# Building the bias table of a neighbourhood attention by transfers through a DRAM scratch and one GpSimd addition, in place of small matmuls

## The reference, cut to what matters

```python
s_loc = jnp.einsum('bhrcqd,bhrcwkd->bhrcqwk', q_blk, k_nb).astype(jnp.float32) * scale
roff = row_idx - r[:, None] + (WIN_ROWS - 1)
coff = jnp.clip(kcol - qcol[:, :, None], -(WIN_COLS - 1), WIN_COLS - 1) + (WIN_COLS - 1)
bias = rpb[:, roff[:, None, None, :, None], coff[None, :, :, None, :]]
s_loc = jnp.where(valid[:, :, None, :], s_loc + bias[None].astype(jnp.float32), NEG_INF)
```

## Time and profile before

| | |
|---|---|
| Median of 3 runs | 1601.49 us (1594.64 to 1602.89) |
| Span of the profiled execution | 1598.6 us |
| PE busy | 1559.7 us, 98% of the span, 8269 matmul records |
| DVE busy | 1197.9 us, 75% |
| ACT busy | 962.1 us, 60% |
| POOL busy | 15.0 us, 1% |
| DMA | 463.38 MB, mean 290 GB/s |
| Mean granted TensorE clock | 0.982 of full speed |

### The profile page before, as it was taken

One profiled execution on the slowest core, in us unless ns is written; L12 is line 12 of the kernel. 1 busy time (PEld: TensorE's weight loads), 2 busy tenths in 40 slices (PEclk: granted clock), 3 DMA queues, 4 the chain that ended last, 5 costly groups with the idle time before them and its releaser, 6 DMA issues.

```text
span 1598.6 us, 21590 instructions
## 1 busy us (share of the span) xinstructions
PE 1559.7 (98%) x8269; PEld 1283.9 (80%) x8269; DVE 1197.9 (75%) x1055; ACT 962.1 (60%) x781; POOL 15.0 (1%) x28
## 2 busy tenths in 40 slices
PE   7999999999999999999999999999999999999997
PEld 3975679899958878888888888888888888888886
DVE  3755457555557578888888888888888888888886
ACT  3422155433444477777777767767767767776774
POOL 1000000000000000000000000000000000000000
PEclk9899999999999899999999999999999999999998
DMA  9745767755546479989989989998999998998990
GB/s 326 253 145 175 239 208 239 251 197 186 183 158 211 158 249 375 374 302 366 368 301 366 373 314 352 370 346 324 376 335 326 375 364 294 370 372 308 370 365 29
DMA packets 221826, 463.38 MB, mean 290 GB/s; under 512 B 7572, under 2 KB 48696, under 8 KB 221768
## 3 DMA queue, kind: packets, MB, share of 16 engines
q1 hardware_dynamic: 220984, 460.84, 80.7%
q0 software_dynamic: 784, 1.75, 0.4%
HBM read 460.98 MB, written 1.57 MB: 289 GB/s over the span
## 4 chain that ended last, share of the span: by engine, by line
PE 94%; DVE 2%; ACT 2%; DMA 1%; issue 0%; SPq 0%; DVEq 0%; ACTq 0%
PE ps L417 92%; PE ps L815 2%; DVE w_lo L1161 1%; ACT hT L1006 1%; DMA raw<-in_ada_w 1%; PE ps L511 1%; DVE rstd L1231 0%; ACT arena L1118 0%; DVE w_lo L1474 0%; ACT w_hi L978 0%; PE ps L594 0%; DVE xT L1481 0%; ACT rnd L1011 0%; DVE tok L1203 0%; SPq L899 0%
## 5 line engine op out<-in xcount | busy, mean ns | idle before, releaser
L417 PE MATMUL ps<-w_hi,rnd 128*128 128x512 f32 x2720 | 868.5, 396 | 2.1 <-DVE rnd L1468 2.1
L1474 DVE TENSOR_TENSOR w_lo<-raw,w_hi 128x2048 fp32r<-128x2048 f32 x335 | 763.5, 2290 | 133.2 <-ACT w_hi L1075 132.7
L1075 ACT ACTIVATE w_hi<-raw 128x2048 fp32r<-128x2048 f32 x336 | 643.5, 1918 | 195.6 <-PE ps L417 195.6
L417 PEld LDWEIGHTS ps<-w_hi,rnd 128*128 128x128 f32 x2720 | 511.8, 188 | 112.7 <-issue 2.3
L417 PE MATMUL ps<-w_lo,rnd 128*128 128x512 f32 x1360 | 530.4, 390 | 0.0
L417 PEld LDWEIGHTS ps<-w_lo,rnd 128*128 128x128 f32 x1360 | 256.1, 188 | 53.3
L417 PE MATMUL ps<-rnd,w_hi 128*128 128x256 f32 x1632 | 293.9, 285 | 4.1 <-DVE rnd L1242 1.7
L417 PEld LDWEIGHTS ps<-rnd,w_hi 128*128 128x128 f32 x1632 | 255.0, 194 | 9.0 <-DVE rnd L1242 3.6
L1161 DVE TENSOR_TENSOR w_lo<-raw,w_hi 128x2048 fp32r<-128x2048 f32 x77 | 175.8, 2285 | 97.9 <-ACT w_hi L978 97.8
L978 ACT ACTIVATE w_hi<-raw 128x2048 fp32r<-128x2048 f32 x77 | 146.6, 1913 | 152.2 <-PE ps L417 143.7
L417 PE MATMUL ps<-rnd,w_lo 128*128 128x256 f32 x816 | 230.5, 282 | 0.0
(11 more groups left out here) (131 smaller groups left out, 717.2 us busy)
## 6 DMA issues: line engine op xcount, KB each, us to landing
raw<-in_moe_w SPq DMA_DIRECT2D x336, 1024.0 KB, 6.9
raw<-in_ada_w SPq DMA_DIRECT2D x48, 1024.0 KB, 5.5
raw<-in_ffn_w SPq DMA_DIRECT2D x33, 1024.0 KB, 5.4
raw<-in_w_in SPq DMA_DIRECT2D x12, 1024.0 KB, 10.5
raw<-in_w_out SPq DMA_DIRECT2D x4, 1024.0 KB, 5.7
raw<-in_fourier_w SPq DMA_DIRECT2D x4, 1024.0 KB, 5.0
out<-tok SPq DMA_DIRECT2D x4, 256.0 KB, 2.1
arena<-dft_constants POOLq DMA_DIRECT2D x1, 640.0 KB, 8.0
```

Source lines behind the costliest of these rows:

```text
L417: return pe.matmul(out, lhsT, rhs, start=first, stop=last, **kw)
L1075: act.activation(w_hi[:, slot, :], raw[:, m % RAW, :], ACT.Copy).then_inc(hi_done, 1)
L1474: dve.tensor_tensor(w_lo[:, slot, :], raw[:, m % RAW, :], w_hi[:, slot, :].bitcast(F32), ALU.subtract).then_inc(lo_done, 1)
```

## The change

The 24 rows of `rpb` no longer go through SBUF and TensorE. GpSimd issues one transfer from DRAM to a DRAM scratch `bias_rows`, which holds the 3 x 31 values of each head 65 times in a row. Then four transfers read it with a row step of 92 elements in place of 93, so that each query column begins one element further to the left, and write the table's four quarters (64 query columns x 8 heads x 64 key columns each) to `bias`. GpSimd waits for them, adds the mask to the whole table in one instruction, and gives `bias_ready`, for which DVE waits in `soften(0)`. TensorE and DVE lose five turns each, `rpbT`, `rpb_rows` and `diag` go, and the router's loads have waits of their own. In the diff the line numbers are left out.

```diff
-CONSTS = [..., ("diag", 2 * GRID_W - 1), ("pair_sum", NG)]
+CONSTS = [..., ("pair_sum", NG)]
+BIAS_COPIES = GRID_W + 1
+    bias_rows = nc.dram_tensor("bias_rows", (HEADS, BIAS_COPIES, BIAS_ROWS * BIAS_COLS), F32, kind="Internal")
```

On TensorE:

```diff
-        def bias_table(q):
-            b = bank()
-            pe.wait_ge(evac_done, rpb_turn)
-            for i in range(16):
-                kc = 16 * q + i
-                last = mm(b[0:GRID_W, 24 * i:24 * (i + 1)], diag[:, GRID_W - 1 - kc:2 * GRID_W - 1 - kc], rpbT[:],
-                          True, True)
-            done(last)
         transposes([kc_tok[:, i * P:(i + 1) * P] for i in range(4)])
-        pe.wait_ge(in_small, 16 * (HEADS + 2))
-        transposes([rpb_rows[:]])
-        rpb_turn = turn[0]
         ada_turn(0, 2, 3)
-        bias_table(0)
-        bias_table(1)
         project("win", h_r, chunk_ready=h_chunk)
-        bias_table(2)
-        bias_table(3)
         project("win", h_r)
         pe.wait_ge(h_ready, 4 * KT)
+        pe.wait_ge(in_small, 32)
```

On GpSimd:

```diff
-        for h in range(HEADS):
-            pool.dma_start(rpb_rows[BIAS_ROWS * h:BIAS_ROWS * (h + 1), :],
-                          ins["rpb"][0, h, WIN_ROWS - 2:WIN_ROWS + 1, :]).then_inc(in_small, 16)
+        rows, row = 2 * WIN_ROWS - 1, BIAS_ROWS * BIAS_COLS
+        near = bass.AP(ins["rpb"].tensor, (WIN_ROWS - 2) * BIAS_COLS,
+                       [[rows * BIAS_COLS, HEADS], [0, BIAS_COPIES], [1, row]])
+        pool.dma_start(bias_rows.ap(), near).then_inc(bias_copied, 16)
         pool.dma_start(router[:], ins["router_w"][0].rearrange("(k p) e -> p k e", p=P)).then_inc(in_small, 16)
         pool.dma_start(router_bias[:], ins["router_b"][0:1, :].to_broadcast([P, EXPERTS])).then_inc(in_small, 16)
+        pool.wait_ge(bias_copied, 16)
+        for qr in range(GRID_R):
+            for kr in range(GRID_R):
+                window = bass.AP(bias_rows, (kr - qr + 1) * BIAS_COLS + WIN_COLS - 1,
+                                 [[row - 1, GRID_W], [BIAS_COPIES * row, HEADS], [1, GRID_W]])
+                pool.dma_start(bias[qr * GRID_W:(qr + 1) * GRID_W, :, kr * GRID_W:(kr + 1) * GRID_W],
+                               window).then_inc(in_bias, 16)
+        pool.wait_ge(in_const, 16)
+        pool.wait_ge(in_bias, 16 * GRID_R * GRID_R)
+        pool.tensor_tensor(bias, bias, mask.rearrange("p (o k) -> p o k", o=1).to_broadcast([P, HEADS, P]),
+                           ALU.add).then_inc(bias_ready, 1)
         round_h(0)
```

On VectorE:

```diff
-        def bias_table(q):
-            b = full()[:, 0:384].rearrange("p (k h r) -> p h k r", h=HEADS, r=BIAS_ROWS)
-            for qr in range(GRID_R):
-                rows = slice(qr * GRID_W, (qr + 1) * GRID_W)
-                for kr in range(GRID_R):
-                    cols = slice(kr * GRID_W + 16 * q, kr * GRID_W + 16 * q + 16)
-                    m = mask[0:GRID_W, cols].rearrange("p (o k) -> p o k", o=1).to_broadcast([GRID_W, HEADS, 16])
-                    last = dve.tensor_tensor(bias[rows, :, cols], b[0:GRID_W, :, :, kr - qr + 1], m, ALU.add)
-            last.then_inc(evac_done, 1)
-        copy_turn(rpbT[:], lambda b: b[0:BIAS_COLS, 0:24])
-        bias_table(0)
-        bias_table(1)
         for c in range(4):
             copy_turn(qT[:, c, :], lambda b: b[:, 0:T])
-        bias_table(2)
-        bias_table(3)
         def soften(h):
+            if h == 0:
+                dve.wait_ge(bias_ready, 1)
             dve.wait_ge(sc_full, h + 1)
```

More of the change, by code:

```diff
@@ L61 @@
 CONSTS = [("ident", P), ("ones", P), ("mask", P), ("earlier", P), ("slot_ids", SLOTS), ("expert_ids", EXPERTS),
-          ("diag", 2 * GRID_W - 1), ("pair_sum", NG)]
+          ("pair_sum", NG)]
 DFT_CONSTS = [("dft_pos", 2 * P), ("dft_cos", 2 * FGC), ("dft_sin", 2 * FGC)]
@@ L191, in _build @@
     router_bias = sb("router_bias", [P, EXPERTS])
-    rpb_rows = sb("rpb_rows", [HEADS * BIAS_ROWS, BIAS_COLS])
-    rpbT = sb("rpbT", [BIAS_COLS, HEADS * BIAS_ROWS])
     small = sb("small", [P, 176])
@@ L259, in _build @@
     ident, ones, mask, earlier = C("ident"), C("ones"), C("mask"), C("earlier")
-    diag = C("diag")[0:BIAS_COLS]
     dft_pos = DFT("dft_pos")
@@ L291, in _build @@
     whole_used = sem("whole_used")
-    in_vec, in_const, in_x, in_cache, in_small, in_dft = (
-        sem(n) for n in ("in_vec", "in_const", "in_x", "in_cache", "in_small", "in_dft"))
+    in_vec, in_const, in_x, in_cache, in_bias, in_small, in_dft = (
+        sem(n) for n in ("in_vec", "in_const", "in_x", "in_cache", "in_bias", "in_small", "in_dft"))
+    bias_copied, bias_ready = sem("bias_copied"), sem("bias_ready")
     mm_done = sem("mm_done")
@@ L1428, in _ @@
         b = full()
+        dve.wait_ge(in_small, 32)
         dve.tensor_tensor(logits, b[:, 0:16].rearrange("p (g e) -> p g e", g=NG),
@@ L1607, in shape_constants @@
     put("expert_ids", np.tile(np.arange(EXPERTS), (P, 1)))
-    u = np.arange(2 * GRID_W - 1)
-    z = (np.arange(BIAS_COLS)[:, None] + u[None, :] == WIN_COLS - 1 + GRID_W - 1).astype(np.float32)
-    put("diag", z)
     angle = 2 * np.pi * (np.outer(i, i) % P) / P
```

## The result

The changed kernel takes 1620.69 us (median of 4 runs, 1616.65 to 1623.9) against 1601.89 us for the kernel before: 1.0138 times as long in the comparison of the runs, with an interval of 1.0107 to 1.0169 (1.0117 by the two medians). The forecast of 1600.5 us and its range to 1611 are missed. The profiled execution has a span of 1619.1 us, 20.5 more than before.

A forecast was written before the change was run, and what follows sets the result against it. TensorE was taken to set the pace, so a shift at the start carries to the end. Terms -4.0 - 1.3 + 0.4 - 0.1 - 1.1 + 4.8 + 0.3 = -1.0 us gave 1600.5 us, range 1595 to 1611.

The forecast's parts named there:

- From there on all is shifted by about -1 us.: Behind L704's successor, everything to the end was to keep its duration and only move by about -1 us.
- the named places: Weight landings, first projection's start, clock between the first two projections, additions near L704's successor: where the forecast would show.
- Second block: Table matmuls at 66.95 to 70.92, ahead of the next projection: removing them counts in full, -4.0 us.
- clock behind it: Projection after the second table matmuls: 12 matmul records no longer run at the lower clock, -1.3 us.
- First block: Table matmuls at 45.90 to 52.2, inside the first norm: covered by the norm's late chunks, so 0.
- clock +0.4: First projection: idle TensorE may keep the clock low longer, 0 to +2.0 us, taken as +0.4.
- Bank rotation: At L704, five turns fewer: TensorE waits for four of VectorE's additions instead of eight, -1.1 us.
- Transfers: At the start, copy (2.5) and windows (0.6 x 4.4) delay the second split half's landing: +4.8 us, ends +1.9 and +9.5.
- GpSimd's addition: Mask addition of 128 x 1024 elements, ending about 42, may slow VectorE's subtractions: 0 to +2.2 us, taken +0.3.
- The late table: Rival: windows land after about 48, so GpSimd's first rounding and the norm wait: +12, 1613 us; chance 0.14.
- The start is not delayed: Rival: small packets fit between weight packets, transfers cost 0.5 and the sum is -5.3: 1596 us; chance 0.10.
- The addition holds VectorE: Rival: a subtraction beside GpSimd's addition waits for all of it, up to 2.5 us: 1603 us; chance 0.06.

The follow-up runs named there:

- e9: Changed kernel plus two unused tensors (512 and 224 bytes), so that every remaining tensor lies at its byte in the kernel before: 1598.99 us, 1.0006.
- e10: e9 with the copy, its windows and the addition issued behind GpSimd's first four roundings instead of ahead of them: 1592.44 us, 0.997.
- e3: Changed kernel with the copy, its windows and the addition behind GpSimd's first four roundings instead of ahead of them: 1613.06 us, 1.0089.
- e4: e3 with an unused tensor of 32 bytes per partition ahead of arena and rnd: 1597.3 us, 0.9983.
- e5: e3 with 224 unused bytes per partition ahead of arena and rnd, so rnd begins 64 past a multiple of 256: 1593.44 us, 0.9964.
- e11: e9 with the scratch's 64 copies (not 65) outermost and its 8 heads inside: 1600.69 us, 1.0004.
- e7: e3 with 160 unused bytes per partition ahead of arena and rnd, so rnd begins at a multiple of 256: 1612.78 us, one run.
- e16: e10 with only the dense stages' regions of rnd 32 bytes further on, at 96 past a multiple of 256: 1598.36 us, 0.9993.
- e12: e9 with the copy still at the start, but the windows and the addition behind GpSimd's first four roundings: 1594.87 us, 0.9984.

## Why the prediction was wrong

**The step that failed** is none of the sum's terms but a sentence behind it: "From there on all is shifted by about -1 us." It took for granted that matmuls that the change doesn't touch keep their duration. With `diag`, `rpb_rows` and `rpbT` gone, the operand of 6528 of the 8140 records had moved. The missing term is +21.7 us (1620.69 against e9's 1598.99). Most of it is in the expert stage, which no edit touches: 15.4 us by the two traces (1021.9 against 1006.5 us from its first record to its last). The prediction named the sign of this: a span more than 8 us off that the named places don't explain. The sum itself holds for e9, where nothing has moved: forecast -1.0 us, measured 1.0006, which is +1.0 us with an interval of -1.3 to +3.0.

Its terms one by one, against e9 where the place would blur them:

- *Second block -4.0, clock behind it -1.3:* right, but half given back by the next term. From the start of the first projection to the next transposes it took 36.26 us before, 32.94 after, 33.05 in e9: -3.2 with the next term, where -4.9 was put down. No stretch between the two projections is at 1.2 GHz now: e9 is at 1.00 from 70 on.
- *First block 0, clock +0.4:* the block was covered, but the clock was mis-sized. With TensorE idle in its place, it stayed at the lower level until the first projection was under way. e10, whose transfers come late, has the same (0.50 in 58.6 to 61), so it isn't their doing. Here is the kernel before by stretch (PE, PEld, DVE, ACT, POOL, then the clock), from the start of its first projection:

```profile
58.00:61.00 3.00, 2.86 (x25) 2.77 (x25) 2.91 (x10) 1.52 (x1) 0.00 (x0) 1.00 0.25 95
61.00:64.00 3.00, 3.00 (x29) 3.00 (x28) 2.43 (x4) 1.92 (x1) 0.00 (x0) 1.00 0.10 21
```

  and e9, whose first projection starts at 63.07:

```profile
57.00:63.00 6.00, 5.19 (x18) 4.26 (x18) 3.90 (x11) 5.91 (x16) 1.21 (x3) 0.50 1.04 369
63.00:66.00 3.00, 2.93 (x13) 2.89 (x14) 1.30 (x3) 2.11 (x2) 0.00 (x0) 0.50 0.27 103
66.00:70.00 4.00, 4.00 (x31) 4.00 (x31) 2.19 (x3) 1.09 (x1) 0.00 (x0) 0.83 0.33 91
```

  Before, 54 records in the first 6 us, 0.11 us each. In e9, 13 + 31 in the first 7, where that rate makes 63: 19 are missing, 19 x 0.11 = 2.1 us. That is the end of my bound, +2.0, where I took +0.4. The reason given, that the clock had risen with the same chunk-paced matmuls, overlooked the 64 small matmuls ahead of them; with those gone the clock rose only in the projection.
- *Bank rotation -1.1:* the count was right, four additions for eight, but the value was low. The chain of the changed kernel at this place:

```profile
452.41 1.14 DVE xT L1363 x4
453.55 0.04 issue
453.59 19.52 PE ps L405 x64
473.11 1.90 PE ps L499 x16
```

  The wait is 1.03 shorter, and the 64 records behind it take 19.52 and not 21.21 us (in e9 too), because the clock no longer falls behind the pause: 0.66 in 445 to 450 before, 1.00 in each 5 us from 445 to 460 now. Together -2.7.
- *Transfers +4.8:* the size was right, the path wasn't. ScalarE takes the second split half at 34.28 in e9, +5.05; TensorE's part starts at 63.07, +4.84, where "near 63" was forecast. The halves of the term were mis-sized, and the errors cancel: the copy 1.5, not 2.5; the windows about 3.3 ahead of that landing, where 0.6 x 4.4 = 2.6 was put down. The first weight half was 4.2 late in e9, not 2. In the profiled execution of the changed kernel the landing is another 1.0 later:

```profile
32.61 1.91 ACT L963 ACTIVATE w_hi<-raw 128x2048 fp32r<-128x2048 f32 x1 [10.45 <-DMA raw<-in_ada_w]
35.31 1.91 ACT L963 ACTIVATE w_hi<-raw 128x2048 fp32r<-128x2048 f32 x1 [0.79 <-DMA raw<-in_ada_w]
```

  In the time, late transfers gave back 7.6, 4.8, 4.9 and 6.5 us in the four pairs (e3, e4, e5, e10). But that each microsecond ahead of the second split half's landing delays everything by one doesn't hold. In e11 this half comes 1.0 us sooner than in e9, and TensorE's part starts 1.2 us later, at 64.25. The chain runs through the end of TensorE's first 48 records, which multiply the first halves whole; in e9 and in e11 it shows them as

```profile
20.01 19.10 PE ps L407 x48
```

```profile
20.05 20.24 PE ps L407 x48
```

  where they took 17.70 before. From their end to TensorE's part it is 23.96 us in e9, 23.97 in e11 and 23.95 in the changed kernel. So e9's +4.84 is +4.2 from the landing of the first weight half and +1.4 from these 48 records, less 0.8 behind them (24.74 before), where TensorE's part now begins one chunk of the norm earlier. By the Trainium skill's rule on the outermost dimension (DMA: Bandwidth & Descriptors, Rules for kernel authors) e11 should have been 0.8 us faster than e9, the prediction's estimate. The trace agrees with the rule as far as it goes: the copy's packets make eight equal shares in e9 (40 of 4464 B and 8 of 1860 B, beside 48 of 48 or 20 B) and sixteen in e11 (32 of 4464 B and 16 of 2976 B), and it came back 1.9 us sooner. The time shows nothing of it within its interval.
- *GpSimd's addition +0.3:* it took 2.34 us, and VectorE had no work beside it. Nothing to pay.

By these readings the sum is +4.8 - 3.2 - 2.7 = -1.1, next to the forecast's -1.0. That is in part luck: two terms were some 2 us off in opposite directions.

The rivals. *The late table* is refuted by GpSimd's timeline (start, duration; after "idle before" what it waited for):

```profile
3.25 0.85 POOL L922 DMA_DIRECT2D bias_rows<-in_rpb  x1
...
11.15 2.73 POOL L930 DMA_DIRECT2D arena<-bias_rows  x4 [5.59 <-DMA bias_rows<-in_rpb]
21.79 2.34 POOL L934 TENSOR_TENSOR arena<-arena,cst 128x1024 f32<-128x1024 f32 x1 [7.90 <-DMA arena<-bias_rows]
59.06 0.40 POOL L913 CAST rnd<-hT 128x256 fp32r<-128x256 f32 x1 [34.93 <-ACT hT L991]
```

The table was ready at 24.1, not 42, with 35 us of cover. Each of the two steps came through the full DMA in 7.6 us. In my model the windows were 2048 packets, 128 for each engine, which would have taken 17.5 us in turn with the weight packets. In the trace they are 128 packets in all, of 4096 B or 16 pieces each, and a packet takes 0.32 us. Of all small transfers in 12 to 22 us (packets, MB, share of 16 engines):

```profile
q0 software_dynamic: 198, 0.52, 26.4%
```

That is 2.6 us of all engines. The price of 51 ns for a piece was that of packets of 180 B on average (225 packets, 0.04 MB) and doesn't apply to pieces that are moved 16 at a time; the higher price of the late table, 0.30 us per piece, even less.

*The start is not delayed:* refuted. *The addition holds VectorE:* not in the changed kernel, where the two didn't meet. In the late versions they overlap, and where the subtraction had begun first it took its usual 2.29 us and GpSimd gave way. The longest overlap is in e7:

```profile
72.63 4.21 POOL L936 TENSOR_TENSOR arena<-arena,cst 128x1024 f32<-128x1024 f32 x1 [6.42 <-DMA arena<-bias_rows]
```

```profile
72.28 2.29 DVE L1147 TENSOR_TENSOR w_lo<-raw,w_hi 128x2048 fp32r<-128x2048 f32 x1 [1.59 <-ACT w_hi L964]
```

The overlap is 1.94 us, and the addition took 1.87 longer than its 2.34 alone. The same shows in e16 (0.99 us, 0.91 longer) and e3 (0.92, 0.84). In e12 the addition had begun first, at 66.54; it took 2.42, and the subtraction that began 0.34 us before its end took 2.50. The Trainium skill (GPSIMD Engine Reference, Key points) speaks of contention with VectorE instructions that have two SBUF inputs, and the traces agree. That VectorE is the one that waits holds only for the one case in which it came second.

## What to carry to other kernels

Adding or removing a tensor moves every tensor behind it, and TensorE's pace can follow. When untouched matmuls show a new mean at the same granted clock, compare the operands' places in SBUF before looking for a cause in the change, and judge the change with pads that put every tensor back. Where one operand feeds most of a kernel, try a few places for it: here 64 B were worth 6 us, and 32 B the wrong way cost 22. And transfers with 35 us of slack should not stand ahead of the first weight loads, which have none.

## What the runs showed of the hardware

- At full clock matmuls of 512 columns follow each other every 227.5 to 233.3 ns as the mean of the expert stage, and those of 256 columns every 113.3 to 120.0 ns, by the place of the stationary operand (512) or the moving one (256) within 256 B. Of the five places tried, the best for the first kind is the worst for the second.
- In two places the 256-column pace has two levels, 4.5 ns apart, that hold over whole stretches of one execution. They switch only within six records of an interruption.
- 0.19 MB from DRAM to DRAM in 520 pieces of 372 B went as 48 packets of 1860 or 4464 B and as many of a few bytes, landed 7.6 us after its issue, and delayed the weight stream beside it by 1.5 us. 0.52 MB in 2048 pieces of 256 B went as 128 packets of 4096 B and delayed it by 3.3 us.
- An addition of GpSimd (2.34 us alone) that started 0.35 us after a subtraction of VectorE took 4.21 us, and the subtraction its usual 2.29.
- Small matmuls in TensorE's idle time were worth about 2 us of clock to the projection behind them, and a pause of 1.14 in place of 2.17 us kept the clock up at L704's successor.
